# A hybrid decoder layer on one core: masks added by 64-row products beside their scores, both kinds of scores ahead of the values, sample work in bunches of one kind

## What is computed

```python
def fox_attend(q, fq, pq, k, v, fk, pk):          # 6 heads of 64
    s = einsum('bqhd,bkhd->bhqk', q, k) * HEAD_DIM ** -0.5
    s = s + swapaxes(fq, 1, 2)[..., :, None] - swapaxes(fk, 1, 2)[..., None, :]
    s = where(pq[:, None] >= pk[None, :], s, -inf)
    return einsum('bhqk,bkhd->bqhd', softmax(s, axis=-1), v)
```

## Time and profile before

| | us |
|---|---|
| median of 3 runs | 732.49 |
| profiled execution | 732.52 |
| span of its trace | 730.8 |
| PE busy | 690.2 (94%) |
| weight loads busy | 545.2 (75%) |
| DVE busy | 414.1 (57%) |
| ACT busy | 243.4 (33%) |
| POOL busy | 144.4 (20%) |

### The profile page before, as it was taken

How to read it: one execution, slowest core, us unless ns; L and a number is a source line. 1 busy time by engine, 2 the same in 40 slices (tenths; PEclk the granted TensorE clock), 3 DMA queues, 4 the chain that set the end, 5 groups by cost and what they waited for, 6 DMA issues and landing times.

```text
span 730.8 us, 12856 instructions
## 1 busy us (share of the span) xinstructions
PE 690.2 (94%) x4958; PEld 545.2 (75%) x4958; DVE 414.1 (57%) x722; ACT 243.4 (33%) x422; POOL 144.4 (20%) x168
## 2 busy tenths in 40 slices
PE   2999999999999999999999998999998999999995
PEld 2789999888888889999999846554554232588884
DVE  4834927472353303179999953536446797455443
ACT  6636442121111345112121233444542384212211
POOL 3044112111111011213121243222320002212210
PEclk9999999999999999999999999999999999999999
DMA  8312103311110032331210687566841050032332
GB/s 256 100 37 59 29 6 67 86 32 30 31 30 2 4 80 93 104 105 30 58 29 1 187 274 252 155 201 190 270 128 54 34 188 1 1 100 73 101 115 87
DMA packets 60757, 67.27 MB, mean 92 GB/s; under 512 B 15188, under 2 KB 50907, under 8 KB 60697
## 3 DMA queue, kind: packets, MB, share of 16 engines
q1 hardware_dynamic: 55529, 51.37, 23.5%
q0 software_dynamic: 5168, 15.08, 6.9%
HBM read 57.71 MB, written 8.68 MB: 91 GB/s over the span
## 4 chain that ended last, share of the span: by engine, by line
PE 70%; DVE 20%; issue 4%; ACT 3%; SPq 2%; DMA 1%; DVEq 0%; ACTq 0%
PE PS L1727 10%; PE PS L1728 8%; PE PS L1729 8%; DVE RA L1403 8%; PE PS L1656 5%; PE PS L1655 5%; PE PS L1657 4%; PE PS L1975 3%; PE PS L1906 3%; PE PS L1992 3%; PE PS L1954 3%; PE PS L2015 3%; DVE rec L1607 2%; DVE wr L1235 1%; DVE RA L1402 1%
## 5 line engine op out<-in xcount | busy, mean ns | idle before, releaser
L1727 PE MATMUL PS<-xh,wh 128*128 128x368 f32 x576 | 202.1, 351 | 0.0
L1728 PE MATMUL PS<-xl,wh 128*128 128x368 f32 x576 | 190.0, 330 | 0.0
L1729 PE MATMUL PS<-xh,wl 128*128 128x368 f32 x576 | 189.7, 329 | 0.0
L558 POOL TENSOR_TENSOR wl<-wr,wh 128x1024 fp32r<-128x1024 f32 x24 | 61.1, 2547 | 312.1 <-ACT wh L913 312.1
L1727 PEld LDWEIGHTS PS<-xh,wh 128*128 128x128 f32 x576 | 108.2, 188 | 6.7 <-issue 1.6
L1728 PEld LDWEIGHTS PS<-xl,wh 128*128 128x128 f32 x576 | 108.3, 188 | 1.7
L1729 PEld LDWEIGHTS PS<-xh,wl 128*128 128x128 f32 x576 | 108.2, 188 | 0.0
L1235 DVE TENSOR_TENSOR wr<-wr,small 128x1024 f32<-128x1024 f32 (+1 forms) x26 | 36.1, 1388 | 45.2 <-DMA wr<-in_w_in_dram 45.1
L1538 DVE CUSTOM_DVE_ANT_0 junk<-PS,RA 128x272 bf16<-128x272 f32 (+9 forms) x84 | 39.1, 507 | 38.5 <-PE PS L1979 28.1
L1403 DVE RECIPROCAL RA<-RA 128x1104 f32<-128x1104 f32 x8 | 56.4, 7054 | 0.3
L1655 PE MATMUL PS<-woh,yh 128*128 128x512 f32 (+1 forms) x144 | 56.2, 391 | 0.0
(11 more groups left out here) (313 smaller groups left out, 1061.8 us busy)
## 6 DMA issues: line engine op xcount, KB each, us to landing
wr<-in_w_in_dram SPq DMA_DIRECT2D x24, 512.0 KB, 3.8
kpage<-in_cache_fox_k_dram SPq DMA_DIRECT2D x64, 192.0 KB, 3.8
pagesB<-in_cache_fox_v_dram POOLq DMA_DIRECT2D x32, 192.0 KB, 3.6
RA<-in_cache_fox_v_dram POOLq DMA_DIRECT2D x32, 192.0 KB, 3.9
YF<-in_x_prompt_dram SPq DMA_DIRECT2D x8, 512.0 KB, 7.1
xres<-in_x_prompt_dram SPq DMA_DIRECT2D x8, 512.0 KB, 3.9
out_y_p_dram<-zout SPq DMA_DIRECT2D x16, 256.0 KB, 2.0
wo_raw_a<-in_w_out_dram SPq DMA_DIRECT2D x6, 512.0 KB, 4.8
```

The lines of the kernel that those rows point to most:

```text
L558: eng.tensor_tensor(low, wr[:, c % 2, :, 0:m], wh[:, c % 2, :, 0:m].bitcast(F32), ALU.subtract).then_inc(wlo_done, 1)
L1727: pe.matmul(out, high, xh[:, k, cols], start=(k == 0), stop=False)
L1728: pe.matmul(out, high, xl[:, k, cols], start=False, stop=False)
L1729: ins = pe.matmul(out, low, xh[:, k, cols], start=False, stop=(k == KT - 1))
```

## The change

The masks. Three new tiles `ident_h`, `mask_neg_h` and `mask_T_h` hold, on each half of the partitions, the identity and the two masks cut into their upper and lower 64 rows ("part" 0 and 1). DVE writes them with twelve copies of 64 rows while chunk 14 of the projections is worked on. Each mask product with 128 rows becomes two products with 64 rows, one for each part, on the rows of the head whose scores it adds to: four matmuls for a unit where there were two.

```diff
+                if c == 14:
+                    dve.wait_ge(consts_set, 4)
+                    for out, full in ((ident_h, identb), (mask_neg_h, mask_neg), (mask_T_h, mask_T)):
+                        for part in range(2):
+                            rows = slice(64 * part, 64 * part + 64)
+                            for to in range(2):
+                                dve.tensor_copy(out[64 * to:64 * to + 64, part, :], full[rows, :]).then_inc(halves_done, 1)
...
             chunk_stored(pe, NCHUNK - 2)
+            pe.wait_ge(halves_done, 12)
...
                 if d0 < c1:
-                    for i in range(2):
-                        ins = pe.matmul(s_head(user, i)[:, d0 - c0:c1 - c0], identb[:, :], mask_neg[:, d0 - q0:c1 - q0],
-                                        start=False, stop=True)
+                    for part in range(2):
+                        for i in range(2):
+                            rows = slice(64 * i, 64 * i + 64)
+                            ins = pe.matmul(s_head(user, i)[:, d0 - c0:c1 - c0], ident_h[rows, part, :],
+                                            mask_neg_h[rows, part, d0 - q0:c1 - q0], start=False, stop=(part == 1))
```

```diff
             now, soon, later = soon, later, []
+            sums = [item for item in now if item[0] == "R" and item[1][0] == "sum"]
+            now = rest + [item for item in now if item not in sums]
+            rest = []
             cost = p2_shape(half, b)[1] / 240 + 0.2
             now.append(("S", ("P2", p, half, b)))
+            upto = len(P1_UNITS) - round(len(P1_UNITS) * max(0, 1 - (n + 1) / 10))
+            while ahead and len(P1_UNITS) - len(ahead) < upto:
+                j, c = ahead.pop(0)
+                if now[-1][1][0] == "P2":
+                    now.append(("S", ("P1", p + 1, j, c)))
+                else:
+                    rest.append(("S", ("P1", p + 1, j, c)))
...
             if behind:
                 now.append(("V", behind))
...
+            now += sums
             behind = (p, half, b)
```

```diff
+        bunches.append(back + keys[:2] + turns[:1])
+        bunches.append(keys[2:4] + turns[1:])
+        bunches.append(keys[4:])
+        bunches.append(attend + loads[:1] + scores[:1])
+        bunches.append(loads[1:] + scores[1:])
```

More of the change, by code:

```diff
@@ L158, in plan @@
     soon, later = [], []
-    behind = None
+    behind, rest = None, []
     for p in range(3):
@@ L169, in plan @@
                     later.append(("R", ("sum", behind[0], behind[1])))
+            now += sums
             behind = (p, half, b)
-            upto = len(P1_UNITS) - round(len(P1_UNITS) * max(0, 1 - (n + 1) / 10))
-            while ahead and len(P1_UNITS) - len(ahead) < upto:
-                j, c = ahead.pop(0)
-                now.append(("S", ("P1", p + 1, j, c)))
-                cost += p1_cost(j, c)
-                if not ahead:
-                    soon.append(("N", p + 1))
-                    later.append(("R", ("rows", p + 1)))
             steps.append((now, cost, 0.0))
     assert not soon and not later
-    samples = sample_steps()
+    samples = sample_bunches()
     ends = len(P1_UNITS) + 2 + 2 * len(P2_UNITS) - SAMPLES_EARLY
     whole = sum(c for _, c, _ in steps[:ends])
-    given, spent, all_samples = 0, 0.0, sum(c for _, _, c in samples)
+    given, spent, all_samples = 0, 0.0, sum(c for some in samples for _, _, c in some)
     order, done, k, behind_samples = [], 0.0, 0, 0
@@ L277, in build @@
         mask_neg = sb("mask_neg", [P, P], BF16)
+        ident_h, mask_neg_h = sb("ident_h", [P, 2, P], BF16), sb("mask_neg_h", [P, 2, P], BF16)
+        mask_T_h = sb("mask_T_h", [P, 2, P], BF16)
         pick_q = sb("pick_q", [TS, 96], BF16)
@@ L1998, in key_scores @@
                 if d1 > 0:
-                    for i in range(2):
-                        ins = pe.matmul(s_head(user, i)[0:w, 0:d1], identb[:, 0:w], mask_T[:, q0 - P * b:q0 - P * b + d1],
-                                        start=False, stop=True)
+                    for part in range(2):
+                        for i in range(2):
+                            rows = slice(64 * i, 64 * i + 64)
+                            ins = pe.matmul(s_head(user, i)[0:w, 0:d1], ident_h[rows, part, 0:w],
+                                            mask_T_h[rows, part, q0 - P * b:q0 - P * b + d1], start=False, stop=(part == 1))
                 ins.then_inc(s_full, 1)
```

35 lines of the change are left out of this document (19 added, 16 removed).

## The result

The changed kernel takes 738.93 us in the median of 20 runs (734.63 to 742.17), the kernel before 735.33 in the median of 20 (731.42 to 744.03). The ratio is 1.005, with a 95% interval of 1.0027 to 1.0072: about half a per cent slower. Ratios and their intervals are estimated from all executions but those in a slower state (one of e0's took 855 us) and not from the medians, so the quotient of two medians can differ from them by up to 0.3%. The prediction had 727.3 us and a gain of 5.2, so it missed by 11.6 us. Some 2.8 us of that are its base: three runs had a median of 732.49, more of them have 735.3. The other 8.8 are the change: 3.6 us lost where 5.2 gained were forecast.

What follows compares the result with a forecast made beforehand. PE, busy 94% of the span, was taken as the bound, but DVE from 586 to 605 us. Of 11.0 us saved on paper, 5.2 stayed after waits: 732.5 to 727.3 us, range 722.5 to 733.

Steps and rivals of the forecast that it cites:

- Terms 1 to 4: PE in the attention: 80 fewer shape changes (7.6 us), covered loads (2.6, 0.8), second-part loads and DVE copies costing 0: 11.0 us.
- The rival that the loads show: Mask products: each second part shows its weight load, 54 x 0.10 us, taking the forecast to 732.7 us; chance 0.06.
- The start: Start of the attention: 0.4 us lost to DVE's maxima for the third P1 unit, 0.7 to K page waits; 1.1 together.
- Adjacent score units: P2 and P1 units sharing two slots: waits for maxima 0.5 us, for the exponential 0.3; 0.8 lost.
- The place of the sums: Sums ahead of sample work: 0.8 us lost at the first, 0 at the second; later parts gain 0.4 and 0.
- 563 to 586 us: Attention up to the split: the reciprocal comes one P1 unit later, so 0.4 us of 1.5 is kept.
- 586 to 605: Attention part where DVE is busy 18.8 of 19 us with the same instructions: 0 of 0.9 us kept.
- The sequence 5 term: Sequence 5: transposes of probabilities follow page transposes without a P2 unit and V between; 1.1 us lost.
- slower: the reciprocal in front of the samples: First two sums: sample scores wait behind 5.3 us of DVE; PE idling all of it gives 737.2 us; chance 0.08.

Runs made afterwards that it cites:

- e0: The changed kernel run once more, against the kernel before: 741.09 us, ratio 1.0073.
- e8: The changed kernel with the sums put back at the head of their step: 731.50 us, ratio 0.9961 to the kernel before.
- e5: The kernel before with P1 units put beside P2 alone, sums still at the step's head: 733.75 us, ratio 0.9999.
- e4: The kernel before with the sums alone moved behind the P1 units of their step, right ahead of the sample items: 744.60 us, ratio 1.0110.
- e16: e4 with three idle PE products in two of its waits for the reciprocal: 737.38 us, ratio 1.0053 to the kernel before.
- e17: e4 run again, beside e16: 742.96 us, ratio 1.0110 to the kernel before.
- e2: The kernel before with the new order of a step alone (P1 units beside P2, sums behind V): 740.33 us, ratio 1.0074.
- e15: The kernel before with DVE's reciprocal of the sums replaced by a copy, division left out: 722.96 us, ratio 0.9840.

## Why the prediction was wrong

*Terms 1 to 4, the saving of 11.0 us with no longer waits.* Right in mechanism and price: 0.10 us for a change of shape, covered first loads, hidden loads of the second parts. The twelve copies take 2.55 us on DVE (2.6 were written), and in e8, which has them, the first P1 unit starts at 412.97 us, before at 413.32: they are hidden. The rival that the loads show is out: masks take 0.12 us to their own shape. By the rule of the Trainium skill that stood beside it, in "TensorE: Matmul & The Clock Gate", section "The mechanism", they should have shown; the trace disagrees.

*The start, 1.1 lost.* Too small. The page waits come to 3.0 us in the changed kernel and to 1.3 before; I had booked 0.7 for a growth of 1.7, which the spread between traces of one kernel (1.5 and 4.5) covers.

*Adjacent score units, 0.8 lost.* As a term of the waits it was mis-sized, as P1 units wait for maxima seven times, 3.7 us in all. As a part of the change it costs nothing that e5 can show (0.9999, give or take 2 us).

*The place of the sums: 0.8 at the first, 0 at the second, +0.4 and 0 behind them.* This is the step that failed. Taken alone, the sums' new place costs 6.5 to 8.2 us in the changed kernel (e8) and 8.1 in the kernel before (e4). I walked the chain from the first sum to the transposes of probabilities, and that end of it came out as written (1.14, 0.40 and 1.00 us idle, where 2.5 were booked). At the second sum 0 were booked and PE's idle time grew by 1.1. What the walk left out is that a sum's reciprocal is 3.35 us of DVE at six places, and that moving all six later puts it ahead of other things that PE needs: the slots of the scores and bank 4.

*563 to 586 us, +0.4, and 586 to 605, 0.* Both too high, and by the same step. PE's waits grew by 1.6 us up to the split, where 1.1 was booked, and by 1.7 from there to the last V of this part, where 0.9 was. I let the reciprocal come one P1 unit later and counted only up to the split; the P2 unit that needs the last P1's slot waits 1.82 us for it (586.11). In the next part I wrote that DVE has the same instructions and so bounds it as before. The same instructions in another order moved V's release behind a reciprocal: 2.75 instead of 1.08 us. That DVE is busy for 18.8 of 19 us doesn't say that another order of the same work can't hurt.

*The sequence 5 term, 1.1.* Right: 1.00 us idle at 521.68.

*The rivals.* The one named "slower: the reciprocal in front of the samples" had the cause, and 0.08. I priced it at two places and dismissed it since PE has 5 us of sample work there. That held for the first place. The case reached further, to the slots and bank 4. That its price, 9.9 us against my sum, is close to the 8.8 missed is luck: it had PE idle for 5.3 us at each of two places, where the trace has 2.5 and 3.2, and waits elsewhere and the clock made up the figure.

*What no term held.* The granted clock. By the ratios about half of what the sums' place costs is time at the lower level behind waits (e16 against e17, with the room named there). I had priced an idle microsecond of PE at one.

Not settled: why three parts that sum to 1.7 us give 5.4 together (or 3.6 by the first ratio), within what the intervals allow; how much of the page waits is the change's; and how much the unfilled waits of the last two places cost in clock.

## What to carry to other kernels

Before moving an item in a list that several engines walk, look for the longest single instruction that the item causes on any engine, and list all that stands behind it there: the rings, slots and banks that it frees, not only its own result. A saving on the busiest engine is kept only between its waits, so test each part alone; here the plainest part gave 4 us, and the part that was meant to add to it took 8. And a wait of 2.4 us or more on PE may cost more than its length: at five of the six places in e2, e4 and e17 where PE waits 2.4 to 2.8 us for the reciprocal, the clock behind it fell.

## What was not expected of the hardware

- A reciprocal of 128 x 512 f32 out of PSUM takes 3.35 us on DVE, a copy of the same 0.69. With copies in place of the six reciprocals the kernel before is 11.8 us faster (e15), although DVE is busy for only 57% of its span.
- Waits of 2.4 us on PE were followed by a granted clock of 0.90 over 17 us and 0.53 over 18 us in one execution, 0.80 and 0.84 in another; with three idle products in them it was 1.00 in both, and the kernel lost 4.2 us less.
- Ln followed by Exp on ACT loaded a table at each, 1.28 us a load, in 12 activations of one kernel.
